# A three-part decoder layer: loops written out, four modulation vectors summed one by one in one-column matmuls, and a new hand-over between the parts

## The reference

```
mod = silu(c) @ ada_w + ada_b          # 9 vectors: shift, scale, gate of each part
x += 1/2 * gate1 * norm(swiglu(norm(x) * (1 + scale1) + shift1))        # 2048 -> 2 x 5504 -> 2048
x +=       gate2 * norm(mixer (norm(x) * (1 + scale2) + shift2))        # 2048 -> 4552 -> heads -> 2048
x += 1/2 * gate3 * norm(swiglu(norm(x) * (1 + scale3) + shift3))
```

## Time and profile before

| what | value |
|---|---|
| runs | 2050.27, 2048.18, 2042.05 us, median 2048.18 |
| span of the profiled execution | 2049.2 us, from its first to its last instruction; its own time is not listed apart from the three runs |
| PE busy | 1914.4 us (93%), mean granted clock 0.959 |
| DVE, ACT, POOL busy | 1440.6 (70%), 821.6 (40%), 39.3 us (2%) |
| DMA | 486 MB, 237 GB/s over the span |
| opening, first part | 0 to 137 us, 137 to 833 us |
| seam 1, mixer's projection | 833 to 854 us, to 1062 us |
| heads, output projection | to 1206 us, to 1291 us |
| seam 2, third part, end | 1291 to 1313 us, to 2036 us, to 2049 us |

### The profile page before, as it was taken

How to read it: one execution, slowest core, us unless ns; L and a number is a source line. 1 busy time by engine, 2 the same in 40 slices (tenths; PEclk the granted TensorE clock), 3 DMA queues, 4 the chain that set the end, 5 groups by cost and what they waited for, 6 DMA issues and landing times.

```text
span 2049.2 us, 23677 instructions
## 1 busy us (share of the span) xinstructions
PE 1914.4 (93%) x8653; PEld 1578.3 (77%) x8653; DVE 1440.6 (70%) x1497; ACT 821.6 (40%) x999; POOL 39.3 (2%) x31
## 2 busy tenths in 40 slices
PE   2589999999999999799998999799999999999996
PEld 1468888888888897578876788688888888888895
DVE  6885788777887766988858566745656665666555
ACT  2134443444344443444434533543444344434442
POOL 0020000000000000100000010100000000000000
PEclk6699999999999999899998989899999999999998
DMA  9976888888888864499910155356666666666552
GB/s 335 367 274 211 303 323 310 309 314 318 325 316 319 316 214 170 167 357 387 372 72 1 49 183 192 111 190 207 234 216 225 212 233 219 216 239 211 189 192 91
DMA packets 201877, 486.14 MB, mean 237 GB/s; under 512 B 7952, under 2 KB 18912, under 8 KB 186720
## 3 DMA queue, kind: packets, MB, share of 16 engines
q1 hardware_dynamic: 200608, 482.75, 66.0%
q10 hardware_dynamic: 992, 2.63, 0.4%
q0 software_dynamic: 224, 0.06, 0.0%
HBM read 483.31 MB, written 2.10 MB: 237 GB/s over the span
## 4 chain that ended last, share of the span: by engine, by line
PE 51%; issue 37%; DVE 7%; DMA 3%; ACT 1%; POOL 1%; SPq 0%; POOLq 0%; DVEq 0%; ACTq 0%
PE ps_u L1156 5%; PE ps_u L1155 5%; PE ps_u L1157 5%; PE ps_g L1155 5%; PE ps_g L1157 5%; PE ps_g L1156 5%; PE ps_t L1155 3%; PE ps_t L1157 3%; PE ps_t L1156 3%; PE ps_y L1155 3%; PE ps_y L1157 3%; PE ps_y L1156 3%; DVE arena L931 2%; DMA ada_raw<-in_ada_w 2%; DMA arena<-in_ada_w 1%
## 5 line engine op out<-in xcount | busy, mean ns | idle before, releaser
L692 DVE TENSOR_TENSOR w_lo<-w_raw,w_hi 128x1024 fp32r<-128x1024 f32 (+2 forms) x632 | 755.7, 1200 | 470.6 <-ACT w_hi L461 470.2
L461 ACT ACTIVATE w_hi<-w_raw 128x1024 fp32r<-128x1024 f32 (+2 forms) x632 | 657.6, 1043 | 922.2 <-PE ps_u L1157 288.6
L1155 PE MATMUL ps_g<-w_hi,xT_hi 128*128 128x512 f32 (+2 forms) x832 | 325.2, 391 | 12.4 <-DVE xT_lo L885 7.1
L1155 PE MATMUL ps_u<-w_hi,xT_hi 128*128 128x512 f32 (+1 forms) x832 | 324.8, 390 | 8.4 <-DVE w_lo L692 8.4
L1157 PE MATMUL ps_g<-w_hi,xT_lo 128*128 128x512 f32 (+2 forms) x832 | 322.8, 388 | 0.0
L1156 PE MATMUL ps_g<-w_lo,xT_hi 128*128 128x512 f32 (+2 forms) x832 | 322.6, 388 | 0.0
L1156 PE MATMUL ps_u<-w_lo,xT_hi 128*128 128x512 f32 (+1 forms) x832 | 322.6, 388 | 0.0
L1157 PE MATMUL ps_u<-w_hi,xT_lo 128*128 128x512 f32 (+1 forms) x832 | 322.3, 387 | 0.0
L702 DVE SCALAR_TENSOR_TENSOR arena<-ada_raw,cond,arena 128x2048 f32<-128x2048 f32 x112 | 262.8, 2346 | 0.9 <-DMA ada_raw<-in_ada_w 0.8
L1155 PEld LDWEIGHTS ps_g<-w_hi,xT_hi 128*128 128x128 f32 x832 | 158.3, 190 | 45.5 <-issue 9.1
L1155 PEld LDWEIGHTS ps_u<-w_hi,xT_hi 128*128 128x128 f32 x832 | 157.5, 189 | 40.1 <-DVE w_lo L692 10.4
(11 more groups left out here) (217 smaller groups left out, 1725.8 us busy)
## 6 DMA issues: line engine op xcount, KB each, us to landing
w_raw<-in_ffn_w_in SPq DMA_DIRECT2D x160, 1024.0 KB, 5.1
ada_raw<-in_ada_w SPq DMA_DIRECT2D x128, 1024.0 KB, 5.0
w_raw<-in_ffn_w_out SPq DMA_DIRECT2D x80, 1024.0 KB, 5.0
w_raw<-in_mix_w_in SPq DMA_DIRECT2D x32, 1024.0 KB, 9.2
arena<-in_ada_w SPq DMA_DIRECT2D x16, 1024.0 KB, 7.4
w_raw<-in_mix_w_out SPq DMA_DIRECT2D x16, 1024.0 KB, 5.1
w_raw<-in_ffn_w_in SPq DMA_DIRECT2D x16, 768.0 KB, 4.4
w_raw<-in_ffn_w_out SPq DMA_DIRECT2D x8, 768.0 KB, 4.3
```

The source lines that it names most:

```text
L461: nc.scalar.activation(w_hi[:, u % 4, 0:n, 0:width], w_raw[:, s, 2 * hf:2 * hf + n, 0:width], ACT.Copy).then_inc(hi_done, 1)
L692: nc.vector.tensor_tensor(w_lo[:, u % 4, 0:n, 0:width], w_raw[:, s, 2 * hf:2 * hf + n, 0:width], w_hi[:, u % 4, 0:n, 0:width].bitcast(F32) ...
L1155: nc.tensor.matmul(o, a_hi[:, k, rows], w_hi[:, b, c, 0:width], start=start, stop=False)
```

## The change

Every `Fori` is written out as a Python loop, on all engines. The modulations now come in a fixed list, one after the other: 3, 4, 2, 6, 7 in the first part (80 steps, one every 2.5 units from its fourth group on), 5 in the mixer's projection (16), 8 in the third part (16, one every 8 units). The steps' places are counted in units (`ada_at`), and their loads stand behind fixed weight loads (`ada_load_at`). `mod_rows` is replaced by `col_sums`: 16 matmuls of one column (a 128x128 piece of `acc` by a column of ones), four times in the first part, behind the transposes of blocks 3, 5, 8 and 10, with one or two small DVE steps to finish. The biases of 3, 4, 6 and 7 come by two more small loads at the start.

At the seams the last addition to y is split by token tile, x is updated in four steps and squared in four, and x is multiplied by its row scale before the transposes, so the diagonal matrix and `rbc` fall away there. The scaling and shifting is one DVE step, the rounding one ACT step of 512 columns. Three pairs are transposed ahead of the next group, the other five behind its units 0 to 4. Fifty 128x128 matmuls on the identity (`warm`) are put where PE would wait. Three units of the next group's `w_lo` stand before the last addition to y.

```diff
+MODS_LATER = ((3, 0), (4, 3), (2, 1), (6, 0), (7, 3), (5, 0), (8, 3))
+SUMMED = (3, 4, 6, 7)
+ADA_FFN1, ADA_MIX, ADA_FFN2 = 0, 5 * KD, 6 * KD
+UNIT_FFN1 = [5 * a // 2 for a in range(5 * KD)]
+UNIT_MIX = [12 + 7 * a // 2 for a in range(KD)]
+UNIT_FFN2 = [16 + 8 * a for a in range(KD)]
+def ada_total(mod):
+    return ADA_PRE + KD * ([m for m, _ in MODS_LATER].index(mod) + 1)
...
+        ada_at = [8 * (G_FFN[0] + 3) + u for u in UNIT_FFN1]
+        ada_at += [8 * G_IN + u for u in UNIT_MIX]
+        ada_at += [8 * G_FFN[1] + u for u in UNIT_FFN2]
+        def ada_load_at(a):
+            first = a in (ADA_FFN1, ADA_MIX, ADA_FFN2)
+            second = a - 1 in (ADA_FFN1, ADA_MIX, ADA_FFN2)
+            if first or second:
+                return max((ada_at[a] - 5) // 2, 4 * (G_FFN[0] + OPENING))
+            return (ada_at[a - 2] + 7) // 2 + 1
...
+            def load_ada(a):
+                mod, k = MODS_LATER[a // KD][0], a % KD
+                sp.wait_ge(ada_done, ADA_PRE + a - 1)
+                sp.dma_start(ada_raw[:, a % 2, :], ada_v[k, :, mod * D:(mod + 1) * D]).then_inc(ada_landed[a % 2], 16)
+            def load_group(g, src_of):
                 for s in range(4):
                     dst, src = src_of(s)
                     sp.wait_ge(lo_done, 8 * g - 8 + 2 * s + 2)
                     sp.dma_start(dst, src).then_inc(w_landed[s], 16)
...
+                    for a in range(len(ada_at)):
+                        if ada_load_at(a) == 4 * g + s:
+                            if a == ADA_MIX:
+                                sp.wait_ge(gates_ready, 1)
+                            if a == ADA_FFN2:
+                                sp.wait_ge(gates_ready, 2)
+                            load_ada(a)
...
-                with sp.Fori(0, LOOP) as i:
-                    hidden(i + 2, g0 + 5 + 3 * i, NB, ada_hook(MODS_FFN[f], ADA_FFN[f], i, 12))
-                hidden(FBLOCKS - 1, g0 + 5 + 3 * LOOP, TAIL, None)
+                    hidden(1, g0 + 2, NB)
+                for i in range(LOOP):
...
+            sp.dma_start(small_rows[6 * KD:8 * KD, :], ada_b[0, 3 * D:5 * D].rearrange("(k p) -> k p", p=P)).then_inc(c_landed, 16)
+            sp.dma_start(more_rows[:, :], ada_b[0, 6 * D:8 * D].rearrange("(k p) -> k p", p=P)).then_inc(c_landed, 16)
...
+            def y_square(n, t, b):
+                return nc.scalar.activation(junk[:, (2 * b + t) % 4 * NB:((2 * b + t) % 4 + 1) * NB],
+                                            yacc[:, t, b * NB:(b + 1) * NB], ACT.Square, accum_out=ssy[:, t, b:b + 1])
+            def y_squares(n, y0, g):
+                for b in range(3):
                     act.wait_ge(y_added, y0 + b + 1)
...
+                    if b == 2:
+                        act.wait_ge(ysq_done, 4 * n + 1)
+                    y_square(n, 0, b)
+                    y_square(n, 1, b).then_inc(ysq_done, 1)
+                    if g is not None and b == 1:
+                        hi_group(g, 4, NB, None, range(0, 2))
+                if g is not None:
+                    hi_group(g, 4, NB, None, range(2, 3))
+                act.wait_ge(ysq_done, 4 * n + 2)
+                act.wait_ge(y_first, n + 1)
+                y_square(n, 0, 3)
+                act.wait_ge(y_added, y0 + 4)
+                y_square(n, 1, 3).then_inc(ysq_done, 1)
...
+                act.wait_ge(ysq_done, 4 * n)
                 for t in range(TILES):
...
+                    for hf in range(2):
+                        act.wait_ge(x_new, 4 * (n - 1) + 2 * t + hf + 1)
+                        if t:
+                            act.wait_ge(xsq_done, 2 + 4 * (n - 1) + hf + 1)
+                        nc.scalar.activation(junk[:, hf * 1024:(hf + 1) * 1024], x_sb[:, t, hf * 1024:(hf + 1) * 1024], ACT.Square,
+                                             accum_out=ssx[:, t, hf:hf + 1]).then_inc(xsq_done, 1)
...
+            def xt_hi_later(n, b):
+                def f():
+                    act.wait_ge(xt_scaled, 8 * n + b + 1)
+                    nc.scalar.activation(xT_hi[:, 2 * b:2 * b + 2, :],
+                                         junk[:, (b % 4) * 2 * SEQ:(b % 4 + 1) * 2 * SEQ].rearrange("p (c n) -> p c n", n=SEQ),
+                                         ACT.Copy).then_inc(xt_hi_done, 1)
+                return f
...
-                hi_group(g, 4, NB, None, range(4))
                 x_squares(n)
-                row_scale(n)
-                for b in range(3):
-                    xt_hi(n, b)()
+                hi_group(g, 4, NB, None, range(3, 4))
+                for b in range(4):
+                    xt_hi_later(n, b)()
...
+                    if 8 * g + u in ada_at:
+                        ada_unit(ada_at.index(8 * g + u))
...
+            def mod_cols(i):
                 def f():
...
+                    n, scale = 1 + i // 2, i % 2
+                    dve.wait_ge(cols_done, STRIPS + i + 1)
+                    ins = nc.vector.tensor_tensor(modcol[:, n, 1 - scale, :], ps_y[:, 0, 0:KD], bias1[:, 2 + i, :], ALU.add)
+                    if scale:
+                        link(ins)
                         ins = nc.vector.scalar_tensor_tensor(modcol[:, n, 0, :], modcol[:, n, 0, :], 1.0, gpre[:, n, :], ALU.add, ALU.mult)
                     ins.then_inc(modcol_done, 1)
                 return f
...
-                y_add(g, y0 + 2, 2)()
                 gated(0)
                 gated(1)
+                if g_next is not None:
+                    lo_group(g_next, 4, NB, None, range(0, 1))
+                y_add(g, y0 + 2, 2)()
+                if g_next is not None:
+                    lo_group(g_next, 4, NB, None, range(1, 2))
                 gated(2)
-                y_add(g, y0 + 3, 3)()
+                if g_next is not None:
+                    lo_group(g_next, 4, NB, None, range(2, 3))
+                last = slice(3 * NB, 4 * NB)
+                dve.wait_ge(y_added, y0 + 3)
+                dve.wait_ge(pe_half, n + 1)
+                nc.vector.tensor_tensor(yacc[:, 0, last], ps_t[:, 0, :], yacc[:, 0, last], ALU.add).then_inc(y_first, 1)
+                dve.wait_ge(pe_used, 8 * g + 8)
+                nc.vector.tensor_tensor(yacc[:, 1, last], ps_t[:, 1, :], yacc[:, 1, last], ALU.add).then_inc(y_added, 1)
...
+            def xt_raw(n, b):
+                dve.wait_ge(xt_done, 8 * n + b + 1)
+                if b >= 4:
+                    dve.wait_ge(xt_lo_done, 8 * n + b - 3)
+                for c in range(2):
+                    k = 2 * b + c
+                    last = nc.vector.tensor_scalar(junk[:, (k % 8) * SEQ:(k % 8 + 1) * SEQ], xt_bank(n, b)[:, c * SEQ:(c + 1) * SEQ],
+                                                   modcol[:, n, 0, k:k + 1], modcol[:, n, 1, k:k + 1], ALU.mult, ALU.add)
+                last.then_inc(xt_scaled, 1)
+            def xt_rest(n, b):
+                dve.wait_ge(xt_hi_done, 8 * n + b + 1)
+                nc.vector.tensor_tensor(xT_lo[:, 2 * b:2 * b + 2, :],
+                                        junk[:, (b % 4) * 2 * SEQ:(b % 4 + 1) * 2 * SEQ].rearrange("p (c n) -> p c n", n=SEQ),
+                                        xT_hi[:, 2 * b:2 * b + 2, :].bitcast(F32), ALU.subtract).then_inc(xt_lo_done, 1)
...
+                dve.wait_ge(xsq_done, 2 + 4 * n)
+                link(nc.vector.reduce_sum(ss[:, 2:4], ssx[:, :, :], AX_X))
+                nc.vector.tensor_scalar(ss[:, 2:4], ss[:, 2:4], 1.0 / D, EPS, ALU.mult, ALU.add).then_inc(var_ready, 1)
+                norms[0] += 1
                 lo_group(g, 4, NB, None, range(3, 4))
...
+                dve.wait_ge(x_new, 4 * n)
+                dve.wait_ge(rstd_ready, norms[0])
+                for hf in range(2):
+                    for t in range(TILES):
+                        cols = slice(hf * D // 2, (hf + 1) * D // 2)
+                        nc.vector.tensor_scalar(yacc[:, t, cols], x_sb[:, t, cols], rstd[:, 2 + t:3 + t], None, ALU.mult).then_inc(xn_ready, 1)
+                dve.wait_ge(modcol_done, 2 * n + 4)
+                for b in range(4):
+                    xt_raw(n, b)
                     if b:
...
+                        xt_rest(n, b - 1)
...
+                    if half is not None and t == 0:
+                        ins.then_inc(half, 1)
...
+            def col_sums(i):
+                pe.wait_ge(ada_done, ada_total(SUMMED[i]))
+                pos = dict(MODS_LATER)[SUMMED[i]]
+                for k in range(KD):
+                    ins = nc.tensor.matmul(ps_y[:, 0, k:k + 1], acc[:, pos, k * P:(k + 1) * P], ones[:, 0:1], start=True, stop=True)
+                ins.then_inc(cols_done, 1)
...
+            def warm(n):
+                for _ in range(n):
+                    nc.tensor.matmul(ps_g[:, 0, 0:P], ident[:, :], ident[:, :], start=True, stop=True)
+            def x_pair(n, b):
+                def f():
+                    pe.wait_ge(xn_ready, 4 * (n - 1) + (2 if b < 4 else 4))
+                    if b >= 6:
+                        pe.wait_ge(xt_scaled, 8 * n + b - 5)
```

(48 more changed lines are left out.)

295 lines of the change are left out of this document (92 added, 203 removed).

## The result

The changed kernel takes 2055.38 us (median of seven runs, 2054.46 to 2056.38) against 2048.18; ratio 1.0033 [1.0022, 1.0045]. It is some 7 us slower, where the forecast was 2.3 us faster.

What follows compares the result with a forecast made beforehand. The prediction took PE's own stream to bound the kernel, with PE waiting only at the seams. Its terms summed to -2.3 us, taking the median from 2048.18 to 2045.9 us, called no change, with a range of 2032 to 2060.

Steps and rivals of the forecast that it cites:

- The step that failed: Column sums in the first part's full stretch: 3.4 us on PE's path at each of four places, +13.6 us.
- Loops written out: All engines: unrolling changes nothing, as PE showed no idle time in the looped stretches; 0 us.
- rivals of instruction supply: PE's longer written-out stream: some 40 further pieces each hold PE 0.5 us; +20 us, 2066, chance 0.07.
- of branches: Loop ends: removing PE's 19 branches saves 1 us each; -19 us, 2027, chance 0.04.
- `mod_rows` out of the projection: Mixer's projection: two whole `mod_rows` fall away from PE's full stretch; -6.9 us.
- the group behind seam 1: First group after the seam: 6.9 us lost before, 4.6 after, to late pairs and clock; -2.3 us.
- Last out group: End of the first part: without `mod_rows` and `mod_cols` it falls from 24.83 to 18.70 us; -6.1 us.
- Modulation steps: First part, 64 to 80 steps: DVE and transfers still fit in a 66 us round; 0 us.
- The late load: First part's rounds: modulation loads late by 4 us make PE wait in nine rounds; 15 us, 2061, chance 0.09.
- Seam 1: PE's wait after the first part: +1.7 us up to the first scalars, -1.9 us from there to the next group.
- Seam 2: PE's wait before the third part: +0.5 us up to the first scalars, -3.6 us from there to the next group.
- Group behind seam 2: First group after the seam: 1.9 us lost before, 4.6 after, to late pairs and clock; +2.7 us.

Runs made afterwards that it cites:

- 5: Changed kernel with the three `w_lo` steps at each seam moved back behind the update of x; ratio 1.0042 to the kernel before the change.
- 6: Changed kernel without the 50 filler matmuls at each of the two seams; ratio 1.0030 to the kernel before the change.
- run 7: Changed kernel with `w_lo` only in DVE's idle slots at the seams and eight more fillers before the next group; 2048.4 us, ratio 1.0006.
- kernels 3: Changed kernel with one column sum in place of 16 at each of the four places; 2037.3 us, ratio 0.9934.
- kernel 8: Changed kernel with three of the four column sums moved to seam 1, 64 columns wide, in place of fillers; 2040.2 us, ratio 0.9962.
- run 10: Changed kernel with idle-slot `w_lo`, more fillers, three sums at seam 1, then later POOL clear, bias additions apart, modulation steps four units later; 2030.2 us, ratio 0.9903.
- run 4: Changed kernel with each one-column sum issued twice, 32 calls a place instead of 16; 2081.5 us, ratio 1.0152.

## Why the prediction was wrong

The step that failed is "8 calls took 1.70 us, `col_sums` has 16, so 3.4 us, four times on PE's path: +13.6". The calls, their place and their number were right; the term measured 23.9 us. In sixteen places with one-column sums in four profiles (the changed kernel, 5, 6 and 7) the price was 3.6 three times, 5.1 to 5.2 seven times and 6.8 six times, 5.5 in the mean. The price per call was read from a row that says what the call takes, and not what it does to the matmuls behind it. With 64 columns the same calls cost 3.57, my price plus a little. In the kernel before I could have read that a full PE can be slow: in the retention stretch it is busy 31.99 of 32.00 us at a clock of 0.68, with matmuls of 64 to 256 columns. I took "PE is full" for "the clock is safe", and no rival named it.

The Trainium skill (TensorE: Matmul & The Clock Gate, "What's actually happening") says that the clock follows how busy the engine has recently been. Run 7 agrees: with 0.51 us of pause instead of 2.29 the matmuls behind it kept 0.40 us. Taken as "busy in the profile" the rule fails here, since 5.00 busy us of 5.00 stood at 0.51.

The other terms, forecast and measured, against the span of 2049.2:

- Loops written out: 0, and 0 (66.18 us in both). The rivals of instruction supply and of branches are out: PE had no gap that the longer stream made.
- `mod_rows` out of the projection and the group behind seam 1: -6.9 and -2.3; together -9.8 measured.
- Last out group: -6.1; -7.7. The sum took the 18.7 us of the third part's; kernels 3 and 8 have them, the changed kernel's profile has 17.1.
- Modulation steps: 0; **+1.5**. The late load was named as a rival with a price in each of nine rounds; it came in one, and run 10 removed it.
- Seam 1: -0.2; +0.2. Seam 2: -3.1; -2.8. Group behind seam 2: +2.7; +3.8. The clock took the 1.6 us of the sum (71.0 less the 69.4 of run 7). The rest is PE waiting for `xT_lo` of the last two pairs (idle 0.33 and 0.78 us in the profile): by the starts of the matmuls around them the two cost 1.6 us, where the sum has 0.6 for one.
- End: -0.5; -0.4, but from the transposes on this stretch lay between 667.1 and 668.7 in profiles of the same code. Opening: +0.5; -1.6, and its mark lay between 178.1 and 180.9. So nothing follows from either, nor from the heads stage, 1.8 us shorter.

The sums' excess of 10.3 us outweighs everything else. Without it the span would have been 2044.3, 2.6 below the forecast; that the rest comes so near is in part luck, since +1.5 (late step) and +1.1 us (group behind seam 2) stand against -1.6 (last out group), -2.1 (opening) and -1.8 (heads).

## What to carry to other kernels

Price a matmul by its row and by the clock of the matmuls behind it: a row of one-column matmuls that keeps PE at 100% can leave it at the 1.2 GHz level, and widening the moving operand from one column to 64 adds next to nothing (the weight loads were busy for 3.90 of 3.90 us inside the one-column row of 442 us). Short rows between full units kept the clock as well. Put such small work where PE waits, and put side steps of DVE only where DVE waits. When times of one kernel lie in two bunches, compare the clock stage by stage between profiles before taking it for noise; here it was worth 9 to 10 us.

## What the runs showed of the hardware

- The width of a narrow fp32 matmul is nearly free up to 128 columns: 96 records of 128x64 took 10.83 us in kernel 8, 0.113 each, 48 records of 128x128 fillers 5.52 in the changed kernel, 0.115, and one-column records 0.106, or 0.174 once the clock has fallen (run 4).
- DVE and POOL hold each other up: POOL's power over 128x2 took 0.70 us alone and 1.60 beside a `w_lo`, and four DVE scalings 2.74 us alone and 4.17 beside a clear by POOL. The Trainium skill (SBUF — State Buffer, "🔬 SBUF: two separate sides") says that the two share a port pair, which one instruction takes for its whole length while the other waits, if DVE's is in a two-port mode, or has two operands in SBUF against one of POOL's that reads SBUF. `w_lo` and the power are the second case, and the power's 0.9 us more agree with it; that the scalings are in such a mode no run here shows, only that they were 1.43 us longer.
- The loss by the clock differs from one execution to the next: the same code at the same place cost 3.6, 5.2 or 6.8 us (the first place in the profiles of kernels 7, 5 and 6).

Seam 1 stays 0.5 us longer with the sums in it than without (19.07 in kernel 10, 18.59 in 7): by DVE's timelines the bias additions take 0.19 us of its chain ahead of the second scalars and 0.38 behind the scalings. What stays open: how narrow a matmul may be in a full row before the clock falls, since widths between 1 and 64 were not tried; and why the loss differs between executions.
